# Index logits of a sparse-attention layer: three rounded products of split operands in place of fp32 products

## The chip, the cores and the metric

One core of a Trainium2 chip runs the whole program. The metric is the device time of one execution in microseconds. Three runs of the kernel before gave 2183.99, 2184.31 and 2185.58 us, median 2184.31 us; a fourth execution, taken by the hardware profiler, took 2184.07 us and its trace spans 2182.3 us from the first to the last instruction. All rows below come from that fourth execution.

## The reference, cut to what matters

The program is a two-layer decoder trunk over 512 tokens of width 1024: feed-forward blocks, a gated linear attention beside a state-space mixer in layer 0, a sparse attention in layer 1 (the odd layer), cross attention and a final norm. The change touches one line of the odd layer's mixer, the index logits:

```python
q, k, v, qi, ki, wi = jnp.split(hn @ w_in, _splits(OD_SIZES), axis=-1)
qi = apply_rope(qi.reshape(Bsz, L, IDX_HEADS, IDX_DIM), cos_i, sin_i)   # 8 heads of 64
ki = apply_rope(ki.reshape(Bsz, L, 1, IDX_DIM), cos_i, sin_i)[:, :, 0]   # one key head
# for each block of 128 queries:
logits = jnp.einsum('bqhd,bsd->bqhs', qib, ki)
score = jnp.einsum('bqhs,bqh->bqs', jax.nn.relu(logits), wib)
score = jnp.where(kpos <= tq, score, -jnp.inf)
_, idx = lax.top_k(score, 128)
```

The scores decide which 128 keys each query sees. Queries of the first block (0 to 127) see all their keys, so logits are computed for the query blocks 1, 2 and 3 only.

## The kernel before, in words

Every large product of the program is made of three products of rounded operands ("fp32r"): a weight w is split into a high part (rounded) and a low part (w minus the high part), the activations x likewise, and `mm3` (L431 to L435) adds high·high, high·low and low·high in PSUM. GpSimd (POOL) splits the weights: for each half of a 128x1024 weight block it makes the high part (L387, a tensor_scalar) and the low part (L394, a subtraction of two SBUF operands). It may split a half of block b once TensorE has done with the same half of block b-2, since there are two slots. Scalar engine (ACT) and Vector engine (DVE) split the activations.

The input projections of the odd layer are 15 "tiles" u = 0 to 14 in the order of `OD_ORDER`: u = 0 is the index key (tile 14, stored twice, in rows 0 to 63 and 64 to 127), u = 1 to 4 are the index queries (tiles 10 to 13, two heads of 64 rows each), u = 5 to 14 are the attention's queries and keys. `tile` runs 8 chunks k = 0 to 7 of three matmuls each, and `beside(k)` puts other work ahead of a chunk.

- The projection goes to a PSUM bank. ACT's `swap(u)` (L1535) copies it with halves exchanged into another bank, DVE's `od_out(u)` multiplies by cosine and sine (L2304, L2305) and adds (L2309) into `Pt[t]` in the arena in SBUF: that is the rotary embedding, and the add increments `rope_done`.
- TensorE's `logit_pair(j)` (L921 to L930) stands ahead of chunk 1 and chunk 5 of the tiles u = 3 to 8, twelve pairs in all. A pair is two fp32 products for two heads of one query block, the one on rows 0 to 63, the other on rows 64 to 127, into banks 0 and 1. By `LOGITS` the widths are 512, 384, 512, 384, 512, 384, 512, 384, 256, 256, 256, 256 keys. Pairs 0 and 1 use the query tile of u = 1, pairs 2 and 3 that of u = 2, pairs 4 and 5 of u = 3, pairs 6 and 7 of u = 4. A pair waits for its tile's `rope_done` and for `idx_acc`, the sums of the pair before.
- ACT's `relu_pair` (L1543) applies the relu in place, DVE's `add_logit` (L2325, L2328) multiplies by the head's weight and adds into the score.
- On ACT the order of one round u is: relu of the even pair of tile u+1, `swap(u)`, relu of the odd pair of tile u+1. In round 0 the four copies of the attention's values (L1556) follow, each of which increments `od_v`; tile u = 2 on TensorE waits for the first of them, tiles 3 to 5 for one more each, since they take over those banks.
- On DVE the order of one round is: two `add_logit`, the two multiplications of `od_out`, two `add_logit`, the add. In round 0 the folding of the rotary table (L2295, L2296) and a copy of the mask (L2367) follow; from u = 5 on, rounds of the top-k search (L2344, L2345).

The order of work is written out by hand, each engine runs its own list, and semaphores join them.

Of the kernel before, what the change touches and what calls it, by code (L numbers as in the profile page):

```python
# [28 lines left out]
F32 = mybir.dt.float32  # L29
F32R = mybir.dt.float32r  # L30
I32 = mybir.dt.int32
ALU = mybir.AluOpType
ACT = mybir.ActivationFunctionType
AX = mybir.AxisListType

P = 128
T = 512
# [57 lines left out]
def od_bank(u):  # L95

    return [1, 0][u] if u < 2 else BANKS[u % 4 - 2]
# [74 lines left out]
OD_ORDER = [14, 10, 11, 12, 13] + list(range(10))  # L172
# [59 lines left out]
def build_trunk(nc, xT, memT, pos, vecs, w_alpha, s5b, s5bt, s5c, blocks, mats, mask, rows, stream, out):  # L232
    with ExitStack() as ctx:  # L233
        def sb(name, shape, dt=F32):
            return ctx.enter_context(nc.sbuf_tensor(name, shape, dt))
# [3 lines left out]
        def S(name):  # L239
            if name not in sems:  # L240
                sems[name] = ctx.enter_context(nc.semaphore(name))
            return sems[name]

        ps = ctx.enter_context(nc.psum_tensor("ps", [P, 8, T], F32))
        h = sb("h", [P, KC, T])
        X = [sb(f"x{i}", [P, KC, 2, T], F32R) for i in range(2)]
# [26 lines left out]
        Pt = [ar[:, i * T:(i + 1) * T] for i in range(16)]  # L273
# [6 lines left out]
        def area(at, n=T):  # L280
            return ar[:, at:at + n]
# [19 lines left out]
        def by_offset(x):  # L301

            return x.rearrange("p (s k) -> p k s", s=STRIDE)
        od_val = area(A_ODV, 2 * T).rearrange("p (t d) -> p t d", t=4)

        def split_p(hd, mc, part):

            return X[hd // 2][:, 4 + 2 * (hd % 2) + mc, part, :]
# [121 lines left out]
        def _(pe):  # L430
# [490 lines left out]
            def logit_pair(j):  # L921
                qb, first = LOGITS[2 * j]
                nk = (qb + 1) * P
                pe.wait_ge(S("rope_done"), first // 2 + 2)
                if j >= 1:
                    pe.wait_ge(S("idx_acc"), 2 * j)
                for e in range(2):
                    r = slice(64 * e, 64 * e + 64)
                    pe.matmul(ps[:, e, 0:nk], Pt[10 + first // 2][r, qb * P:(qb + 1) * P],
                              Pt[14][r, 0:nk], start=True, stop=True).then_inc(S("logit_mm"), 1)  # L930

            def odd_inputs():

# [237 lines left out]
        def _(act):  # L1171
# [352 lines left out]
            def swap(u):  # L1524

                i, b = u, od_bank(u)
                n = 64 if OD_ORDER[u] < 10 else 32
                act.wait_ge(S("block_done"), od_block(u) + 1)
                if i >= 2:
                    act.wait_ge(S("rope_done"), i - 1)  # L1530
                if i == 1:
                    act.wait_ge(S("rcol_ready"), 2)
                for at in range(0, P, 2 * n):
                    for lo, up in ((at, at + n), (at + n, at)):
                        m = act.activation(ps[lo:lo + n, 6 + i % 2, :], ps[up:up + n, b, :], ACT.Copy)  # L1535
                m.then_inc(S("rope_s"), 1)

            def odd_inputs():
                def relu_pair(j):
                    for i in (2 * j, 2 * j + 1):  # L1540
                        nk = (LOGITS[i][0] + 1) * P
                        act.wait_ge(S("logit_mm"), i + 1)
                        act.activation(ps[:, i % 2, 0:nk], ps[:, i % 2, 0:nk], ACT.Relu).then_inc(S("relu"), 1)  # L1543

                for u in range(OD_TILES):
                    j = 2 * (u + 1 - LOGIT_TILES[0])
                    if u + 1 in LOGIT_TILES:
                        relu_pair(j)
                    swap(u)
                    if u + 1 in LOGIT_TILES:  # L1550
                        relu_pair(j + 1)
                    if u == 0:
                        act.wait_ge(S("rcol_ready"), 2)
                        for tt in range(4):
                            act.wait_ge(S("wi_ready"), tt + 1)
                            act.activation(od_val[:, tt, :], ps[:, BANKS[tt], 0:2 * P],  # L1556
                                           ACT.Copy, scale=col[:, 16 + tt:17 + tt]).then_inc(S("od_v"), 1)
# [130 lines left out]
            ffn(2, lambda: memory_split(1))  # L1688
            norm(5)
            odd_inputs()  # L1690
            kv_next[0] = 0
            attention(lambda n: fill(1, n))
# [12 lines left out]
        def _(dve):  # L1705
            step = [0]

            def chain(ins):

                step[0] += 1  # L1710
                ins.then_inc(S("dve_step"), 1)
                dve.wait_ge(S("dve_step"), step[0])
# [187 lines left out]
            def rstd_columns(l):  # L1900
                dve.wait_ge(S("rcol_mm"), l + 1)
                dve.tensor_copy(col[:, 16:20], ps[:, RCOL_BANK[l], :].rearrange("p (t n) -> p t n", n=P)[:, :, 0]
                                ).then_inc(S("rcol_ready"), 1)
                dve.wait_ge(S("rcol_ready"), l + 1)
# [384 lines left out]
            def fold(kind):  # L2289

                if kind == 2:
                    dve.wait_ge(S("tab"), 4)
                sign = vec[:, V_SIGNA + kind // 2:V_SIGNA + kind // 2 + 1]
                c, s = area(A_TAB + kind * T), area(A_TAB + (kind + 1) * T)
                dve.tensor_tensor(c, c, rstd[:], ALU.mult)  # L2295
                chain(dve.scalar_tensor_tensor(s, s, sign, rstd[:], ALU.mult, ALU.mult))  # L2296

            def od_out(u, between=None):

                t, src = OD_ORDER[u], ps[:, od_bank(u), :]  # L2300
                i, kind = u, 0 if t < 10 else 2
                turned = ps[:, 6 + i % 2, :]
                dve.wait_ge(S("rope_s"), i + 1)
                dve.tensor_tensor(Pt[t], src, area(A_TAB + kind * T), ALU.mult).then_inc(S("proj_out"), 1)  # L2304
                chain(dve.tensor_tensor(turned, turned, area(A_TAB + (kind + 1) * T), ALU.mult))  # L2305
                if between is not None:
                    between()
                dve.wait_ge(S("proj_out"), OD_BASE + u + 1)
                dve.tensor_tensor(Pt[t], Pt[t], turned, ALU.add).then_inc(S("rope_done"), 1)  # L2309

            def indexer_weights():
                for tt in range(4):
                    dve.tensor_scalar(col[:, 32 + 8 * tt:40 + 8 * tt], ps[:, BANKS[tt], 2 * P:2 * P + WI],
                                      col[:, 16 + tt:17 + tt], (IDX_HEADS * IDX_DIM) ** -0.5, ALU.mult, ALU.mult
                                      ).then_inc(S("wi_ready"), 1)
                dve.wait_ge(S("wi_ready"), 4)

            def add_logit(i):
                qb, hd = LOGITS[i]
                nk = (qb + 1) * P  # L2320
                sc, x = area(A_SC + qb * T)[:, 0:nk], ps[:, i % 2, 0:nk]
                w = col[:, 32 + 8 * qb + hd:33 + 8 * qb + hd]
                dve.wait_ge(S("relu"), i + 1)
                if hd == 0:
                    ins = dve.tensor_scalar(sc, x, w, None, ALU.mult)  # L2325
                else:
                    dve.wait_ge(S("idx_acc"), i)
                    ins = dve.scalar_tensor_tensor(sc, x, w, sc, ALU.mult, ALU.add)  # L2328
                ins.then_inc(S("idx_acc"), 1)
                if hd == IDX_HEADS - 1:  # L2330
                    dve.wait_ge(S("idx_acc"), i + 1)
                    chain(dve.tensor_tensor(sc[:, qb * P:nk], sc[:, qb * P:nk], cmask, ALU.add))
# [18 lines left out]
            def odd_inputs():  # L2351
                fold(2)
                rstd_columns(1)
                indexer_weights()
                for u in range(OD_TILES):
                    first = 4 * (u + 1 - LOGIT_TILES[0])
                    if u + 1 in LOGIT_TILES:
                        add_logit(first)
                        add_logit(first + 1)
                    def later_pair():  # L2360
                        add_logit(first + 2)
                        add_logit(first + 3)

                    od_out(u, later_pair if u + 1 in LOGIT_TILES else None)
                    if u == 0:
                        fold(0)
                        chain(dve.tensor_copy(area(A_SC)[:, 0:P], cmask))  # L2367
                    if u + 1 in LOGIT_TILES:
                        if u >= 5:
                            topk(1)  # L2370
                    elif 8 <= u < 14:
                        topk(2)
# [282 lines left out]
```

## Time and profile before

| what | value |
|---|---|
| median of three runs | 2184.31 us |
| profiled execution: time, span | 2184.07 us, 2182.3 us |
| TensorE (PE) busy | 2169.7 us, 99% of the span |
| weight loads (PEld) busy | 1793.2 us, 82% |
| GpSimd (POOL) busy | 1533.1 us, 70% |
| Vector (DVE) busy | 1045.5 us, 48% |
| Scalar (ACT) busy | 452.1 us, 21% |
| TensorE in the logit pairs (L929) | 11.0 us busy in 48 records, from 1482.4 to 1525.4 us |

In this trace an fp32 matmul leaves two records and an fp32r matmul one, so a logit pair shows as four. A matmul record lasts from its start to the modelled end of its results, and records overlap; what a matmul costs TensorE is the distance from one start to the next. Times in the rows are microseconds from the start of the span.

### The profile page before, as it was taken

How to read it: one execution, taken by the hardware profiler on the slowest of the kernel's cores; microseconds unless marked ns; L12 is line 12 of the kernel's file. 1: busy time of each engine (PE TensorE's matmuls, PEld its weight loads, DVE VectorE, ACT ScalarE, POOL GpSimd, SP SyncE). 2: the span in 40 equal slices, each digit the busy share in tenths (PEclk: the TensorE clock that was granted, in tenths of full speed). 3: DMA queues.
4: the chain of work that ended last, by engine and by line, in shares of the span. 5: the costliest groups of instructions: out<-in, count | busy, mean ns of one | idle time of the engine just before them, and what ended most of it. 6: DMA issues, size and time to landing. Idle time of an engine off the chain costs nothing. (4 is left out here: it accounts for less than half of the span.)

```text
span 2182.3 us, 30340 instructions
## 1 busy us (share of the span) xinstructions
PE 2169.7 (99%) x10582; PEld 1793.2 (82%) x10582; DVE 1045.5 (48%) x1386; ACT 452.1 (21%) x808; POOL 1533.1 (70%) x1538
## 2 busy tenths in 40 slices
PE   9999999999999999999999999999999999999998
PEld 7888888888888888888888888886878888888887
DVE  6556795695444352233363224346872543222333
ACT  3101212034123210001131111134362332111112
POOL 7777787667964776676777667675756657666764
PEclk9999999999999999999999999999999999999999
DMA  5333333223331323323333333232322223332232
GB/s 193 96 96 115 115 98 122 88 78 98 126 97 54 102 97 96 97 96 97 114 97 96 96 97 97 98 99 77 106 88 92 77 65 95 97 96 97 99 97 82
DMA packets 115350, 214.12 MB, mean 98 GB/s; under 512 B 12832, under 2 KB 14400, under 8 KB 115008
## 3 DMA queue, kind: packets, MB, share of 16 engines
q1 hardware_dynamic: 111024, 202.03, 29.1%
q10 hardware_dynamic: 4240, 10.99, 1.5%
q8 instruction: 49, 0.80, 0.2%
q14 instruction: 37, 0.30, 0.0%
HBM read 208.77 MB, written 4.19 MB: 98 GB/s over the span
## 5 line engine op out<-in xcount | busy, mean ns | idle before, releaser
L433 PE MATMUL ps<-x,w_split 128*128 128x512 f32 (+1 forms) x2854 | 1105.7, 387 | 3.4 <-POOL w_split L394 1.8
L435 PE MATMUL ps<-x,w_split 128*128 128x512 f32 (+1 forms) x2854 | 1097.1, 384 | 0.0
L434 PE MATMUL ps<-x,w_split 128*128 128x512 f32 (+1 forms) x2854 | 1096.9, 384 | 0.0
L394 POOL TENSOR_TENSOR w_split<-w_raw,w_split 128x512 fp32r<-128x512 f32 x758 | 1024.7, 1352 | 63.3
L387 POOL TENSOR_SCALAR w_split<-w_raw 128x512 fp32r<-128x512 f32 x758 | 498.5, 658 | 562.0 <-PE ps L435 555.2
L433 PEld LDWEIGHTS ps<-x,w_split 128*128 128x128 f32 x2854 | 536.0, 188 | 121.9 <-issue 10.5
L434 PEld LDWEIGHTS ps<-x,w_split 128*128 128x128 f32 x2854 | 536.2, 188 | 106.6 <-issue 1.4
L435 PEld LDWEIGHTS ps<-x,w_split 128*128 128x128 f32 x2854 | 536.1, 188 | 106.6
L1854 DVE TENSOR_TENSOR x<-arena,x 128x512 fp32r<-128x512 f32 x88 | 118.6, 1358 | 219.1 <-ACT x L1306 219.1
L1804 DVE TENSOR_TENSOR tu<-ps,rstd 128x512 f32<-128x512 f32 x88 | 60.7, 689 | 315.7 <-PE ps L435 315.7
L1244 ACT ACTIVATE sg<-tg 128x512 f32<-128x512 f32 x88 | 55.6, 632 | 669.9 <-DVE tg L1801 668.7
L1801 DVE TENSOR_TENSOR tg<-ps,rstd 128x512 f32<-128x512 f32 x88 | 60.6, 689 | 175.2 <-PE ps L435 174.5
L1810 DVE TENSOR_TENSOR arena<-sg,tu 128x512 f32 (+1 forms) x88 | 119.7, 1360 | 17.9 <-ACT sg L1244 9.8
L1306 ACT ACTIVATE x<-arena 128x512 fp32r (+1 forms) x88 | 54.2, 629 | 348.4 <-PE ps L435 348.0
L1769 DVE SCALAR_TENSOR_TENSOR h<-ps,h 128x512 f32<-128x512 f32 x63 | 43.2, 686 | 166.2 <-PE ps L435 165.9
L1174 ACT ACTIVATE x<-h,vec 128x512 fp32r<-128x512 f32 x64 | 46.0, 723 | 221.2 <-DVE h L1769 173.8
L1727 DVE SCALAR_TENSOR_TENSOR x<-h,vec,x 128x512 fp32r<-128x512 f32 x64 | 60.4, 947 | 27.3 <-ACT x L1174 27.3
L433 PE MATMUL ps<-w_split,x 128*128 128x256 f32 (+2 forms) x192 | 59.8, 312 | 0.4 <-POOL w_split L394 0.3
L435 PE MATMUL ps<-w_split,x 128*128 128x256 f32 (+2 forms) x192 | 57.7, 301 | 0.0
L434 PE MATMUL ps<-w_split,x 128*128 128x256 f32 (+2 forms) x192 | 57.6, 300 | 0.0
L1785 DVE RECIPROCAL rstd<-std 128x512 f32<-128x512 f32 x8 | 26.8, 3354 | 53.0 <-ACT std L1234 53.0
L1211 ACT ACTIVATE sq<-h 128x512 f32<-128x512 f32 x63 | 38.9, 618 | 15.2 <-DVE h L1769 15.2
(301 smaller groups left out, 1329.3 us busy)
## 6 DMA issues: line engine op xcount, KB each, us to landing
w_raw<-in_stream SPq DMA_DIRECT2D x758, 256.0 KB, 2.6
arena<-in_memT ACTq DMA_DIRECT2D x2, 1024.0 KB, 4.9
s_tables<-kv ACTq DMA_DIRECT2D x4, 512.0 KB, 3.2
arena<-s_tables ACTq DMA_DIRECT2D x4, 512.0 KB, 4.5
out<-h ACTq DMA_DIRECT2D x6, 256.0 KB, 2.3
h<-in_xT SPq DMA_DIRECT2D x4, 256.0 KB, 5.4
h<-in_xT SPq DMA_DIRECT2D x2, 512.0 KB, 7.0
w_raw<-in_stream SPq DMA_DIRECT2D x5, 128.0 KB, 5.9
```

The costliest lines, as they stand in the source:

```text
L387: pool.tensor_scalar(W[:, s, 0, c], raw[:, s, c], 1.0, 0.0, ALU.mult, ALU.add).then_inc(S(f"w_hi{'ab'[half]}"), 1)
L394: pool.tensor_tensor(lo, x, hi.bitcast(F32), ALU.subtract).then_inc(split_ready if half else S("half_split"), 1)
L433: pe.matmul(dst, wh, xh, start=start, stop=False)
L434: pe.matmul(dst, wh, xl, start=False, stop=False)
L435: return pe.matmul(dst, wl, xh, start=False, stop=stop)
L1244: act.activation(sg[:, s, :], tg[:, s, :], ACT.Silu).then_inc(S("silu"), 1)
L1306: act.activation(X[xo][:, ch:ch + 1, 0, :], hid[:, d, :], ACT.Copy).then_inc(S("x_hi"), 1)
L1727: dve.scalar_tensor_tensor(X[to][:, k, 1, :], h[:, k, :], gain(n, k), X[to][:, k, 0, :].bitcast(F32), ALU.mult, ALU.subtract).then_inc(S(" ...
L1801: dve.tensor_tensor(tg[:, s, :], ps[:, BANKS[2 * s], :], rstd[:], ALU.mult).then_inc(S("gate_ready"), 1)
L1804: dve.tensor_tensor(tu[:, s, :], ps[:, BANKS[2 * s + 1], :], rstd[:], ALU.mult).then_inc(S("up_ready"), 1)
L1810: dve.tensor_tensor(dst, sg[:, s:s + 1, :], tu[:, s:s + 1, :], ALU.mult).then_inc(S("hid_done"), 1)
L1854: dve.tensor_tensor(X[xo][:, ch:ch + 1, 1, :], hid[:, d, :], X[xo][:, ch:ch + 1, 0, :].bitcast(F32), ALU.subtract).then_inc(S("x_lo"), 1)
```

## The change

It touches three places. TensorE's `logit_pair` waits for a new semaphore `idx_lo` in place of `rope_done`, and makes six fp32r matmuls of a pair in place of two fp32 ones: three products (high·high, low·high, high·low) for each of the two heads, heads alternating. The operands are the high and low parts of the index keys and queries, kept in `X[0]`, of which the queries hold only the 384 columns of the blocks 1 to 3. ACT makes the high part in rounds u = 0 to 4, after the relus of the round, as a copy from the arena once the tile's `rope_done` has come; in round 0 it stands ahead of the four value copies. DVE makes the low part as a subtraction of two SBUF operands, after `od_out(u)`, once the high part is there.

```diff
+        def index_split(t, part):
+            x = X[0][:, 0:4, :, :].rearrange("p a b t -> p (a b t)")
+            if t == 14:
+                return x[:, part * T:(part + 1) * T]
+            at = 2 * T + ((t - 10) * 2 + part) * 3 * P
+            return x[:, at:at + 3 * P]
+
+        def index_tile(t):
+            return Pt[t] if t == 14 else Pt[t][:, P:T]
...
             def logit_pair(j):
                 qb, first = LOGITS[2 * j]
                 nk = (qb + 1) * P
-                pe.wait_ge(S("rope_done"), first // 2 + 2)
+                pe.wait_ge(S("idx_lo"), first // 2 + 2)
                 if j >= 1:
                     pe.wait_ge(S("idx_acc"), 2 * j)
-                for e in range(2):
-                    r = slice(64 * e, 64 * e + 64)
-                    pe.matmul(ps[:, e, 0:nk], Pt[10 + first // 2][r, qb * P:(qb + 1) * P],
-                              Pt[14][r, 0:nk], start=True, stop=True).then_inc(S("logit_mm"), 1)
+                for i, (pq, pk) in enumerate(((0, 0), (1, 0), (0, 1))):
+                    for e in range(2):
+                        r = slice(64 * e, 64 * e + 64)
+                        m = pe.matmul(ps[:, e, 0:nk], index_split(10 + first // 2, pq)[r, (qb - 1) * P:qb * P],
+                                      index_split(14, pk)[r, 0:nk], start=(i == 0), stop=(i == 2))
+                        if i == 2:
+                            m.then_inc(S("logit_mm"), 1)
...
                     if u + 1 in LOGIT_TILES:
                         relu_pair(j + 1)
+                    if u < 5:
+                        act.wait_ge(S("rope_done"), u + 1)
+                        act.activation(index_split(OD_ORDER[u], 0), index_tile(OD_ORDER[u]), ACT.Copy
+                                       ).then_inc(S("idx_hi"), 1)
                     if u == 0:
                         act.wait_ge(S("rcol_ready"), 2)
                         for tt in range(4):
...
                     od_out(u, later_pair if u + 1 in LOGIT_TILES else None)
+                    if u < 5:
+                        t = OD_ORDER[u]
+                        dve.wait_ge(S("idx_hi"), u + 1)
+                        dve.tensor_tensor(index_split(t, 1), index_tile(t), index_split(t, 0).bitcast(F32), ALU.subtract
+                                          ).then_inc(S("idx_lo"), 1)
                     if u == 0:
                         fold(0)
```

How the lists of instructions change. Lines of the changed kernel have other numbers: L1550 is the swap (L1535 before), L1558 the relu (L1543), L1575 the value copies (L1556), L1569 the new copy; L2387 is the new subtraction, L2328 the rotary add (L2309 before), L2323 and L2324 the rotary multiplications.

On the Scalar engine before, from the swap of u = 0 to the relus of pair 2:

```order
334 L1535 ACTIVATE ps<-ps 32x512 [waits block_done]
335 L1535 ACTIVATE ps<-ps 32x512 x3
336 L1556 ACTIVATE arena<-ps,col 128x256 [waits wi_ready,rcol_ready]
337 L1556 ACTIVATE arena<-ps,col 128x256 [waits wi_ready] x3
338 L1535 ACTIVATE ps<-ps 32x512 [waits rcol_ready,block_done]
339 L1535 ACTIVATE ps<-ps 32x512 x3
340 L1543 ACTIVATE ps<-ps 128x512 [waits logit_mm] x2
341 L1535 ACTIVATE ps<-ps 32x512 [waits rope_done,block_done]
342 L1535 ACTIVATE ps<-ps 32x512 x3
343 L1543 ACTIVATE ps<-ps 128x384 [waits logit_mm] x2
344 L1543 ACTIVATE ps<-ps 128x512 [waits logit_mm] x2
```

The same stretch in the changed kernel:

```order
334 L1550 ACTIVATE ps<-ps 32x512 [waits block_done]
335 L1550 ACTIVATE ps<-ps 32x512 x3
336 L1569 ACTIVATE x<-arena 128x512 [waits rope_done]
337 L1575 ACTIVATE arena<-ps,col 128x256 [waits wi_ready,rcol_ready]
338 L1575 ACTIVATE arena<-ps,col 128x256 [waits wi_ready] x3
339 L1550 ACTIVATE ps<-ps 32x512 [waits rcol_ready,block_done]
340 L1550 ACTIVATE ps<-ps 32x512 x3
341 L1569 ACTIVATE x<-arena 128x384 [waits rope_done]
342 L1558 ACTIVATE ps<-ps 128x512 [waits logit_mm] x2
343 L1550 ACTIVATE ps<-ps 32x512 [waits rope_done,block_done]
344 L1550 ACTIVATE ps<-ps 32x512 x3
345 L1558 ACTIVATE ps<-ps 128x384 [waits logit_mm] x2
```

The first new copy waits for the rotary add of the key and stands ahead of the value copies; the copy of u = 2 comes next after the last row shown, behind the relus of pair 1.

On the Vector engine in the changed kernel, from the rotary add of u = 0 to the subtraction of u = 2:

```order
706 L2328 TENSOR_TENSOR arena<-arena,ps 128x512 [waits proj_out,dve_step]
707 L2387 TENSOR_TENSOR x<-arena,x 128x512 [waits idx_hi]
708 L2314 TENSOR_TENSOR arena<-arena,rstd 128x512
709 L2315 SCALAR_TENSOR_TENSOR arena<-arena,vec,rstd 128x512
710 L2391 COPY arena<-mat 128x128 [waits dve_step]
711 L2323 TENSOR_TENSOR arena<-ps,arena 128x512 [waits rope_s,dve_step]
712 L2324 TENSOR_TENSOR ps<-ps,arena 128x512
713 L2328 TENSOR_TENSOR arena<-arena,ps 128x512 [waits proj_out,dve_step]
714 L2387 TENSOR_TENSOR x<-arena,x 128x384 [waits idx_hi]
715 L2344 TENSOR_SCALAR arena<-ps,col 128x512 [waits relu]
```

Before, the rows were the same without the two of L2387. In rounds 2 to 4 the subtraction follows the add in the same way and is the last instruction of the round.

## Rows read from the trace of the kernel before

**Rows 1.** The page: busy time by engine, then the granted clock in 40 slices.

```profile
PE 2169.7 (99%) x10582; PEld 1793.2 (82%) x10582; DVE 1045.5 (48%) x1386; ACT 452.1 (21%) x808; POOL 1533.1 (70%) x1538
...
PEclk9999999999999999999999999999999999999999
```

**Rows 2.** Timeline, PE, pair 0 (512 keys): start, length, engine, line, operation.

```profile
1482.04 0.39 PE L435 MATMUL ps<-x,w_split 128*128 128x512 f32 x1
1482.36 1.13 PE L929 MATMUL ps<-arena 64*128 64x512 f32 x4
1483.42 0.50 PE L433 MATMUL ps<-x,w_split 128*128 128x512 f32 x1
1483.75 0.39 PE L434 MATMUL ps<-x,w_split 128*128 128x512 f32 x1
```

**Rows 3.** Timeline, PE, pairs 1 (384 keys), 2 and 11 (256 keys).

```profile
1486.38 0.92 PE L929 MATMUL ps<-arena 64*128 64x384 f32 x4
1487.22 0.50 PE L433 MATMUL ps<-x,w_split 128*128 128x512 f32 x1
...
1489.87 0.39 PE L435 MATMUL ps<-x,w_split 128*128 128x512 f32 x1
1490.26 0.70 PE L929 MATMUL ps<-arena 64*128 64x512 f32 x2
...
1524.65 0.70 PE L929 MATMUL ps<-arena 64*128 64x256 f32 x4
1525.28 0.50 PE L433 MATMUL ps<-x,w_split 128*128 128x512 f32 x1
```

**Rows 4.** Timeline, PE, a run of fp32r matmuls of 256 columns.

```profile
1620.42 0.28 PE L433 MATMUL ps<-w_split,x 128*128 128x256 f32 x1
...
1622.81 0.28 PE L435 MATMUL ps<-w_split,x 128*128 128x256 f32 x1
```

**Rows 5.** Waits of PEld: who was waited for, us in total, times, longest.

```profile
PEld ps L929 <- DVE arena L2309: 1.3, 3, 0.4
```

**Rows 6.** Timeline, PE, the first matmul of tile u = 2.

```profile
1476.15 0.39 PE L433 MATMUL ps<-x,w_split 128*128 128x512 f32 x1
```

**Rows 7.** Timeline, ACT, u = 0 to the relus of pair 1; then line L1306.

```profile
1474.16 1.57 ACT L1556 ACTIVATE arena<-ps,col 128x256 f32<-128x256 f32 x4 [1.46 <-DVE col L2313]
1476.35 2.29 ACT L1535 ACTIVATE ps<-ps 32x512 f32<-32x512 f32 x4 [0.62 <-PE ps L435]
...
1487.32 0.86 ACT L1543 ACTIVATE ps<-ps 128x384 f32<-128x384 f32 x2 [0.42 <-PE ps L929]
...
L1306 ACT ACTIVATE x<-arena x88: 615/632/634, 243.1 to 2148.0; 128x512 fp32r x64, 128x512 fp32r<-128x512 f32 x24
```

**Rows 8.** Timeline, DVE, u = 0 to 1, and the end of round 2.

```profile
1475.83 0.69 DVE L2309 TENSOR_TENSOR arena<-arena,ps 128x512 f32<-128x512 f32 x1
1476.43 0.68 DVE L2295 TENSOR_TENSOR arena<-arena,rstd 128x512 f32<-128x512 f32 x1
...
1479.40 0.69 DVE L2304 TENSOR_TENSOR arena<-ps,arena 128x512 f32<-128x512 f32 x1
...
1480.73 0.69 DVE L2309 TENSOR_TENSOR arena<-arena,ps 128x512 f32<-128x512 f32 x1
...
1489.53 0.68 DVE L2309 TENSOR_TENSOR arena<-arena,ps 128x512 f32<-128x512 f32 x1
```

**Rows 9.** Timeline, POOL, the split beside pair 2.

```profile
1489.73 0.62 POOL L387 TENSOR_SCALAR w_split<-w_raw 128x512 fp32r<-128x512 f32 x1 [1.82 <-PE ps L435]
1490.44 1.26 POOL L394 TENSOR_TENSOR w_split<-w_raw,w_split 128x512 fp32r<-128x512 f32 x1
```

**Rows 10.** Line L1854 on DVE (ns min/median/max); then DVE and POOL timelines, one collision.

```profile
L1854 DVE TENSOR_TENSOR x<-arena,x x88: 677/1772/1784, 243.8 to 2148.6; 128x512 fp32r<-128x512 f32 x88
...
2099.90 1.78 DVE L1854 TENSOR_TENSOR x<-arena,x 128x512 fp32r<-128x512 f32 x1 [3.66 <-ACT x L1306]
...
2099.85 1.28 POOL L394 TENSOR_TENSOR w_split<-w_raw,w_split 128x512 fp32r<-128x512 f32 x1
```

## The prediction

> **What bounds the kernel now.** I read the busy times first: TensorE is busy for 99% of the span at a granted clock of nine tenths or more in every slice [rows 1]. So almost every us that TensorE loses is a us of the time, and an engine at 48% (DVE) or 21% (ACT) costs nothing until TensorE has to wait for it. Next I read the TensorE timeline around the logit pairs, since the change lives there. A full fp32r matmul of 512 columns costs 0.2265 us from start to start (26 steps from 1476.15 to 1482.04) [rows 2, 6]; one of 256 columns costs 0.1195 us (20 steps) [rows 4]. Last I read who keeps TensorE waiting there: PEld waited for the rotary add L2309 three times, 0.4 us each [rows 5]. Part of that is the usual gap: the step from the last fp32r matmul to pair 0 is 0.32 us, to pair 2 it is 0.39 us [rows 2, 3]. The real wait before pairs 2, 4 and 6 is thus near 0.1 us each, 0.3 us in all. It is small, but it says that **the chain through relu, score sums and rotary add already ends last at those three pairs**. What the change puts behind that add comes straight onto TensorE's path.
>
> **Part 1: the matmuls of a pair.** Before, pair 0 takes 0.32 us to switch in, 1.06 us from its start to the next matmul, then 0.33 us for a step that otherwise takes 0.23 [rows 2]. The 1.06 us are 0.84 at 384 keys and 0.63 at 256 [rows 3]. The two differences, 0.22 and 0.21 us for 128 columns each, say 1.7 ns for a column: four passes at 2.4 GHz (the higher level of the clock), and four, not eight, because the two heads on rows 0 to 63 and 64 to 127 run side by side. What is left is a fixed 0.20 us. After, there are six one-pass matmuls. If the halves run side by side too, these are three rounds at 0.2265, 0.17 (between the two measured widths) and 0.1195 us; with the same 0.20 us a pair has 0.88, 0.71 and 0.56 us, which saves 0.18, 0.13 and 0.07 us. Four pairs of each: **-1.5 us in all**. No half-row fp32r matmul is in the trace, so I bound it from both sides. Good end: the 0.10 us of the slow step behind a pair go too, another 1.2 us, so -2.7. Bad end: no side-by-side at all, six matmuls of 0.2265, 0.17 and 0.1195 us plus 0.20, which is 1.56, 1.22 and 0.92 us and costs 0.50, 0.38 and 0.29 more, **+4.7 us** over twelve pairs. I take -1.5, since the fp32 halves on the same rows do overlap.
>
> Here a page speaks against the forecast. The Trainium skill, "TensorE: Matmul & The Clock Gate", section "The mechanism", says that a weight load overlaps matmuls in flight only where the row group differs; the six matmuls load each row group three times, so by that rule two loads of each pair would be exposed. The 0.10 us of late start behind a pair is the nearest measure of one exposed load [rows 2]; with it a mechanism of its own follows, the fifth case below.
>
> **Part 2: the key's copy and subtraction (u = 0).** The first copy of ACT waits for the rotary add of the key, which ends at 1475.83 + 0.69 = 1476.52 [rows 8]. It is 512 columns SBUF to SBUF, 0.63 us as L1306 [rows 7]: done 1477.19. Queued behind it are the four value copies, 0.39 us each, which started at 1474.16 [rows 7] and now start at 1477.19. The first is done at 1477.58. Tile u = 2 needs it and began at 1476.15 [rows 6]; it now begins near 1477.6. **+1.5 us.** The next three value copies are wanted a tile later each, and cost nothing. POOL is late by nothing: its splits wait for TensorE.
>
> **Part 3: pair 0 waits for the query of u = 1.** ACT: the last value copy ends 1478.75, swap(1) takes 2.29 us [rows 7], until 1481.05. DVE: the key's subtraction starts at 1477.2; what followed the add took from 1476.43 to 1479.40 [rows 8], 2.97 us, so DVE is there at about 1480.9 if the subtraction takes 0.7 us, and 1481.7 if it stands behind POOL. Then the two multiplications and the add, 1479.40 to 1481.42 [rows 8], 2.02 us: 1483.1. Copy of 384 columns: 0.63 minus about 0.11 (the relu's 1.07 us for two of 512 against 0.86 for two of 384), so 0.53: 1483.65. Subtraction, 0.56 alone: 1484.3, with a short wait behind POOL's L387 1484.45. TensorE is ready for the pair at 1482.36 + 1.5 = 1483.85. **+0.7 us**, and +2.0 if either subtraction falls behind a whole L394.
>
> **Part 4: pairs 2, 4 and 6.** This is the largest term. In round u of DVE the rotary add ends the chain; pair 1 starts at 1486.38, the add of round 2 ends at 1489.53 + 0.68 = 1490.21, pair 2 starts at 1490.26 [rows 3, 8]. Behind the add now come the copy on ACT (0.04 of signal, 0.53) and the subtraction on DVE. The pair itself is 0.13 us shorter. So the subtraction can start at 1490.21 + 0.04 + 0.53 + 0.04 - 0.13 = 1490.69 on the old scale, while TensorE would be ready at 1490.17 - 0.13 = 1490.04. That is 0.65 us late already. And POOL is in the way: its L394 runs from 1490.44 to 1491.70 [rows 9], released by the end of tile u, 0.13 less on the same scale, 1490.31 to 1491.57. Both subtractions read two SBUF operands. What happens then is in the trace: L1854, the same instruction at 512 columns, takes 0.68 us alone and 1.77 us in the median; the one at 2099.90 began 0.05 us behind an L394 of 1.28 us, and ended 0.55 us after it [rows 10]. So the new subtraction waits until 1491.57, ends 0.45 us later (384 columns), 1492.02, and TensorE starts at 1492.07: 2.0 us after it was ready. The same phases repeat for pairs 4 and 6, because POOL and the chain both hang on the same tile. **3 x 2.0 = +6.1 us**, in place of the 0.3 us waited now. Were there no collision, the subtraction would end at 1491.25 and a wait would be 1.25 us, 3.8 us in all.
>
> A page gives the rule for this row: the Trainium skill, "SBUF — State Buffer", section "Who interferes with whom", says that a DVE instruction with two SBUF inputs and a GpSimd instruction that reads SBUF exclude each other, the later one blocked entirely, and that issue order decides. The row agrees (1.78 us); by the opposite order DVE would pay nothing.
>
> **Part 5: what is free.** Pairs 8 to 11 and the odd ones use tiles that were split before: no new wait. The five copies and subtractions, some 3 and 3 to 6 us of work, fill engines that now stand idle, outside the places counted. No DMA is added. POOL may be held up by a subtraction for up to 0.7 us, against 1.82 us for which it sat idle before such a split [rows 9]. Later stages start late by the same amount on all engines, and nothing is made up, since TensorE is the bound.
>
> **Sum.** +1.5 +0.7 +6.1 -0.3 -1.5 = **+6.5 us** on the profiled execution's 2184.07 us (span 2182.3), that is 2190.6 us. That execution is 0.24 us under the median of the three runs, 2184.31, against which I read faster and slower; it makes +6.3.
>
> **Rivals.**
> 1. Forecast: slower by about 6 us, 2190.6. Chance 0.55.
> 2. The waits come but the port collision does not, because DVE gets there first or the phases shift, and the switch behind a pair gets cheap: 6.5 - 2.3 - 1.2 = +3.0, 2187.1. For: the phase margin between copy and L394 is a few tenths of a us. Against: 1.77 us is the median of 88 such subtractions [rows 10]. Chance 0.18.
> 3. Half rows don't run side by side in fp32r: the pairs cost +4.7 in place of -1.5, 6.5 + 6.2 = +12.7, 2196.8. For: no such instruction in the trace. Against: the fp32 pairs overlap, and 128 columns cost them 0.21 us, not 0.43. Chance 0.08.
> 4. Faster: the new work lies off the chain altogether, no wait (the 0.3 us go too), and the whole fixed cost of a pair, 0.20 + 0.10 + 0.09 us of switching in, belongs to fp32 and goes: -0.3 - 1.5 - 12 x 0.39 = -6.5, 2177.6. It decides only if the copy and subtraction end before TensorE is ready, which the 0.65 us of part 4 forbid before any collision. Chance 0.05.
> 5. Loads of one row group exposed twice a pair: 12 x 0.2 = 2.4 more, 2193.0. Against: full fp32r matmuls load the same rows each time and still step at 0.2265 us. Chance 0.09.
> 6. The change saves the pair's time but hardly costs: chain as in 2 with single waits hidden, within 3 us of before. Chance 0.05.
>
> **How the numbers follow.** 0.2% is 4.4 us, about what a measurement of this kernel can tell from no change: slower is above 2188.7. Cases 1, 3 and 5 are above, with a little taken off for case 1's lower tail: 0.72 - 0.02 = 0.70, and a fifth of case 2: 0.73 in all. Case 4 gives faster, 0.05. The rest, 0.22, is no change. The range: its low end is case 2's, 2187.0; its high end is 2195.0, over case 5 with pair 0's longer wait (+1.3), and leaves case 3 out. Some 0.1 lies below and 0.1 above.
>
> **What would show it.** Right: TensorE idle near 1.5 us at the first matmul of tile u = 2; an idle of about 2 us before pairs 2, 4 and 6 put down to L2387; L2387 at 384 columns lasting over 1 us in rounds 2 to 4, with an L394 beside it; a pair of 512 from its start to the next matmul at 0.88 us. The forecast is wrong if L2387 lasts 0.56 us there (case 2), if a pair takes 1.5 us (case 3), or if TensorE doesn't wait at those places (cases 4 and 6). If the granted clock falls to 1.2 GHz behind one of the waits, which no wait of up to 2 us in this trace tests in that stretch, every matmul there takes twice as long and the time is some us above the sum.

## The result and the profile after

The changed kernel took 2192.91 us (median of seven runs, 2191.47 to 2194.73) against 2184.54 us for the kernel before in the same seven rounds (2183.99 to 2186.07): 1.0038 times, 95% interval 1.0028 to 1.0047, or 8.4 us more. The forecast was 2190.6 us, range 2187 to 2195, slower. The profiled execution is one of 2192.91 us with a span of 2191.1 us.

On the page the busy times hardly move: TensorE 2172.5 us, still 99%, and DVE 1050.8 against 1045.5 [rows 1]. The loss can't be seen there. It is in the waits of TensorE; the first view holds those of the changed kernel (who waits, for whom, us in total, times, longest):

```profile
PE ps L942 <- DVE x L2387: 5.2, 4, 1.9
PE ps L445 <- POOL w_split L406: 1.9, 2, 1.6
PE ps L445 <- ACT arena L1575: 1.5, 1, 1.5
```

The first row is the pairs waiting for the new subtraction, the third is tile u = 2 waiting for the value copies. Before, PE had no wait in this stretch and its weight loads waited 1.3 us for the rotary add [rows 5]. The second row stands before as well, at the start of the program.

The timeline of TensorE, with idle time and its releaser in brackets, answers to [rows 2, 3, 6]:

```profile
1476.09 0.39 PE L447 MATMUL ps<-x,w_split 128*128 128x512 f32 x1
1477.99 0.47 PE L445 MATMUL ps<-x,w_split 128*128 128x512 f32 x1 [1.52 <-ACT arena L1575]
...
1483.99 0.39 PE L447 MATMUL ps<-x,w_split 128*128 128x512 f32 x1
1484.94 0.96 PE L942 MATMUL ps<-x 64*128 64x512 f32 x6 [0.56 <-DVE x L2387]
1485.83 0.50 PE L445 MATMUL ps<-x,w_split 128*128 128x512 f32 x1
...
1488.78 0.79 PE L942 MATMUL ps<-x 64*128 64x384 f32 x6
1489.49 0.50 PE L445 MATMUL ps<-x,w_split 128*128 128x512 f32 x1
...
1492.12 0.39 PE L447 MATMUL ps<-x,w_split 128*128 128x512 f32 x1
1494.43 0.96 PE L942 MATMUL ps<-x 64*128 64x512 f32 x6 [1.92 <-DVE x L2387]
...
1501.61 0.39 PE L447 MATMUL ps<-x,w_split 128*128 128x512 f32 x1
1503.92 1.20 PE L942 MATMUL ps<-x 64*128 64x512 f32 x6 [1.92 <-DVE x L2387]
1505.05 0.79 PE L445 MATMUL ps<-x,w_split 128*128 128x512 f32 x1
1505.64 0.63 PE L446 MATMUL ps<-x,w_split 128*128 128x512 f32 x1
...
1512.66 0.39 PE L447 MATMUL ps<-x,w_split 128*128 128x512 f32 x1
1513.83 0.97 PE L942 MATMUL ps<-x 64*128 64x512 f32 x6 [0.79 <-DVE x L2387]
...
1532.48 0.50 PE L445 MATMUL ps<-x,w_split 128*128 128x512 f32 x1
```

Read steps from start to start, not the bracket alone. The step to tile u = 2 is 1.90 us in place of 0.23: 1.7 us lost. The steps to pairs 0, 2, 4, 6 are 0.95, 2.31, 2.31 and 1.17 us where 0.32 is the plain switch: 0.6, 2.0, 2.0 and 0.85 us lost. A pair itself, from its start to the next matmul, is 0.89 us at 512 keys and 0.71 at 384, against 1.06 and 0.84 [rows 2, 3]. The last line is the matmul behind pair 11, 7.2 us later than before (1525.28) [rows 3].

Behind pair 4 the matmuls step at 0.43 us, not 0.23. The granted clock of these stretches (columns: stretch, length, busy time of the five engines, clock, DMA share, GB/s) says why:

```profile
1502.00:1504.00 2.00, 0.08 (x2) 0.09 (x2) 1.27 (x2) 0.52 (x1) 1.36 (x2) 1.00 0.00 0
1504.00:1506.00 2.00, 2.00 (x8) 1.23 (x9) 0.24 (x1) 0.85 (x2) 0.00 (x0) 0.61 0.50 131
1506.00:1508.00 2.00, 2.00 (x6) 1.54 (x5) 1.26 (x2) 1.94 (x5) 0.00 (x0) 0.53 0.00 0
1508.00:1510.00 2.00, 2.00 (x12) 1.24 (x11) 1.30 (x2) 0.54 (x1) 1.08 (x2) 1.00 0.00 0
```

TensorE idled from 1502.0 to 1503.9. It then still had the full clock until about 1504.4 (0.91 in the stretch from 1504.25 to 1504.5), and the lower level, 1.2 GHz, until about 1507.9 (0.50 from 1505 to 1507.5). From pair 4 to pair 5 it took 5.38 us, from pair 0 to pair 1 3.84: 1.5 us lost. Then the wait at pair 6 came out shorter. The rotary adds and subtractions of rounds 2 and 4 on DVE, and their neighbours on POOL, in the changed kernel:

```profile
1491.95 0.68 DVE L2328 TENSOR_TENSOR arena<-arena,ps 128x512 f32<-128x512 f32 x1
1493.21 1.16 DVE L2387 TENSOR_TENSOR x<-arena,x 128x384 fp32r<-128x384 f32 x1 [0.59 <-ACT x L1569]
...
1511.95 0.68 DVE L2328 TENSOR_TENSOR arena<-arena,ps 128x512 f32<-128x512 f32 x1
1513.22 0.56 DVE L2387 TENSOR_TENSOR x<-arena,x 128x384 fp32r<-128x384 f32 x1 [0.59 <-ACT x L1569]
...
1492.69 1.26 POOL L406 TENSOR_TENSOR w_split<-w_raw,w_split 128x512 fp32r<-128x512 f32 x1
...
1513.23 1.69 POOL L406 TENSOR_TENSOR w_split<-w_raw,w_split 128x512 fp32r<-128x512 f32 x1
```

In round 2 POOL came first, by 0.52 us, and DVE's subtraction lasted 1.16 us; in round 4, after the slow clock, DVE was first by 0.01 us: its subtraction took 0.56 us and POOL's stretched from 1.26 to 1.69. That is 0.6 us of the 1.1 by which the step to pair 6 is shorter (1.17 against 2.31). The other 0.5 comes from the chain itself. The slow clock held up TensorE alone, so DVE had its two multiplications of the round done before pair 5's relus came, and began pair 5's score sums 1.39 us after the pair's start (1510.69 against 1509.30) where it was 1.91 us behind pair 1 (1490.69 against 1488.78). The rotary add thus starts 0.71 us ahead of TensorE's last matmul before pair 6, and only 0.17 us ahead of the one before pair 2.

The books of the profiled execution, in us: +1.7 (tile u = 2), +0.6, +2.0, +2.0, +0.85 (pairs 0, 2, 4, 6), +1.5 (clock), -0.3 (old waits), -1.5 (twelve pairs, 0.17, 0.13 and 0.08 each) make 6.85. The two traces are 7.2 us apart at the norm behind this stretch (mean-square matmuls at 1714.8 against 1707.6) and 0.2 at the one ahead (1466.5 against 1466.3), so 7.0 us arise between. The rest of the 8.8 us between the spans is in the last microseconds of the program, the sixteen small matmuls of the final norm, first the changed kernel, then the one before:

```profile
2180.13 3.66 PE L484 MATMUL ps<-mat,col 128*128 128x128 f32 x16
```

```profile
2172.90 2.05 PE L472 MATMUL ps<-mat,col 128*128 128x128 f32 x16
```

The same matmuls take 1.6 us more at the lower clock (granted 0.50 from 2181 to 2183 us; 1.00 from 2173 to 2175 in the kernel before), in code that the change doesn't touch. Among the profiles of the experiments below, x4's has the same fall at the final norm (3.45 us), all others take 2.05 us there. A fall can come elsewhere too. The profile of x11, which has no copy and no subtraction, was taken of an execution 1.8 us over that kernel's lowest, and has its fall near 25 us, behind a wait for a split weight:

```profile
24.23 0.50 PE L433 MATMUL ps<-x,w_split 128*128 128x512 f32 x1 [1.77 <-POOL w_split L394]
24.57 0.41 PE L434 MATMUL ps<-x,w_split 128*128 128x512 f32 x1
24.81 0.59 PE L435 MATMUL ps<-x,w_split 128*128 128x512 f32 x1
25.20 0.63 PE L433 MATMUL ps<-x,w_split 128*128 128x512 f32 x1
```

The kernel before waits 1.84 us at the same place and its profile has no fall. So falls of some 1.5 us each come in some executions and not in others, which fits the groups some 1.5 us apart in which the times of one kernel lie (2191.5, 2192.6 to 2193.0, 2194.5 to 2194.7 here). No profile of the kernel before caught an execution of its upper groups, so for that kernel it is not shown.

### The profile page after: what moved, and what is told of

It reads as the page before. It is cut to its first block and busy times, and to the rows that moved or that the text cites. A ratio compares the mean times of both kernels' runs of the same rounds, so it can differ in the third digit from the quotient of the medians.

```text
span 2191.1 us, 30398 instructions
## 1 busy us (share of the span) xinstructions
PE 2172.5 (99%) x10606; PEld 1798.0 (82%) x10606; DVE 1050.8 (48%) x1391; ACT 454.9 (21%) x813; POOL 1535.8 (70%) x1538
```

## The experiments

Eleven kernels besides. My theory: the products save 1.5 us; all of the loss is TensorE waiting for operands that the chain relu, score sums, rotary add, copy, subtraction delivers late, made worse by the collision with POOL's subtraction and by the clock behind a wait. Rivals: the half-row products themselves cost; the copies and subtractions cost wherever they stand.

**x1_products_alone: the new matmuls, nothing else.** The kernel before with

```diff
-                    pe.matmul(ps[:, e, 0:nk], Pt[10 + first // 2][r, qb * P:(qb + 1) * P], Pt[14][r, 0:nk], ...)
+                for i, (pq, pk) in enumerate(((0, 0), (1, 0), (0, 1))):
+                    for e in range(2): ...
+                        m = pe.matmul(ps[:, e, 0:nk], X[1][r, 0, pq, (qb - 1) * P:qb * P], X[1][r, 1, pk, 0:nk], ...)
```

> The kernel before with the six half-row rounded products of a pair, but on other operands that lie ready (parts of the projection's input), behind the old wait for the rotary add; no copies, no subtractions. The logits are therefore not the index logits. It prices the matmuls alone. My account (the pair's time is one pass of four less, the chain untouched): pairs of 0.89, 0.71 and 0.54 us to the next matmul in place of 1.06, 0.84 and 0.63, the waits before pairs 2, 4, 6 the same 0.1 us, together -1.5 us: 2183.0, ratio 0.9993. Rival (half rows cost more in their new form than fp32, and the trace of the changed kernel hides it in its waits): +0 to +5 us.

2183.41 us, ratio 0.9994 (0.9985 to 1.0003), before 2185.08 in the same session. The interval holds no change; the trace is what prices it. Its pair 0 (timeline, TensorE):

```profile
1482.42 0.39 PE L435 MATMUL ps<-x,w_split 128*128 128x512 f32 x1
1482.74 0.97 PE L930 MATMUL ps<-x 64*128 64x512 f32 x6
1483.64 0.50 PE L433 MATMUL ps<-x,w_split 128*128 128x512 f32 x1
1483.98 0.40 PE L434 MATMUL ps<-x,w_split 128*128 128x512 f32 x1
```

0.32 us in, 0.90 to the next, then 0.34: the fixed costs of the fp32 pair stayed, one pass of four went. The products are no part of the loss, as I expected. The waits did not stay the same, though: the steps to pairs 2, 4 and 6 are 0.56, 0.52 and 0.56 us where the kernel before has 0.39 to 0.41, so 0.4 of the 1.5 us comes back as waiting for the rotary add. No run follows that up.

**x2_waits_alone: the new waits, old matmuls.** The changed kernel with the fp32 lines put back under the wait for `idx_lo`.

```diff
-                for i, (pq, pk) in enumerate(((0, 0), (1, 0), (0, 1))): ...
+                for e in range(2): ...
+                    pe.matmul(ps[:, e, 0:nk], Pt[10 + first // 2][r, qb * P:(qb + 1) * P], Pt[14][r, 0:nk], ...)
```

> The changed kernel with the old fp32 pairs, but behind the new waits, with all copies and subtractions. My account (all of the loss is the chain): the loss of the changed kernel plus the 1.5 us of the pairs, +8 to +11 us by whether the clock falls behind a wait, ratio 1.004 to 1.005; 2 us of wait before pairs 2 and 4. Rival (the split products themselves cost): clearly less than the changed kernel, near +3.

2193.59 us, ratio 1.0041 (1.0027 to 1.0055). Pairs 2, 4 and 6 now all wait the full length:

```profile
1477.85 0.47 PE L445 MATMUL ps<-x,w_split 128*128 128x512 f32 x1 [1.52 <-ACT arena L1572]
1484.81 1.13 PE L941 MATMUL ps<-arena 64*128 64x512 f32 x4 [0.56 <-DVE x L2384]
...
1494.62 1.13 PE L941 MATMUL ps<-arena 64*128 64x512 f32 x4 [1.92 <-DVE x L2384]
...
1504.43 1.13 PE L941 MATMUL ps<-arena 64*128 64x512 f32 x4 [1.92 <-DVE x L2384]
...
1514.22 1.13 PE L941 MATMUL ps<-arena 64*128 64x512 f32 x4 [1.91 <-DVE x L2384]
```

The waits alone give the whole loss; "clearly less than the changed kernel" did not come. With all waits in place and a granted clock of 1.00 through this stretch the profiled run took 2192.25 us, 8.2 us over the profiled run of the kernel before; by steps the waits make 1.7 + 0.6 + 3 x 2.0 - 0.3 = 8.0.

**x3_values_first: the key's copy behind the value copies.**

```diff
-                    if u < 5: ... act.activation(index_split(OD_ORDER[u], 0), index_tile(OD_ORDER[u]), ACT.Copy)
                     if u == 0: ... four value copies
+                    if u < 5: ... act.activation(index_split(OD_ORDER[u], 0), index_tile(OD_ORDER[u]), ACT.Copy)
```

> The changed kernel with the four value copies ahead of the key's copy on the Scalar engine. My account: the first matmul of tile u = 2 follows its predecessor by 0.23 us as before, -1.6 us; pairs 2, 4, 6 wait as in the changed kernel, 2191.3. Rival (tile u = 2 waits for something else, the port or the bank): no change at tile u = 2.

2193.68 us, ratio 1.0039 (1.0026 to 1.0053), where I had expected 2191.3: a miss. Tile u = 2 starts without a wait, as expected, but the next wait took it all:

```profile
1485.71 0.96 PE L942 MATMUL ps<-x 64*128 64x512 f32 x6 [2.67 <-DVE x L2387]
```

Pair 0 waits 2.67 us in place of 0.56. TensorE came 1.7 us sooner, its operands didn't; and POOL, released sooner too, now ran into DVE's work of round 0 (1.09 and 1.20 us in this version against 0.74 and 0.23 us in the changed kernel for the second table instruction and the mask copy). The two are waits on one chain, and I had read the first as a price of its own. Its profile also has two falls of the clock, behind this wait (granted 0.50 from 1488 to 1490 us) and behind the 1.92 us before pair 6.

**x4_sum_in_psum: one SBUF operand in the subtraction.** The rotary sum of the index tiles stays in PSUM.

```diff
-                dve.tensor_tensor(Pt[t], Pt[t], turned, ALU.add).then_inc(S("rope_done"), 1)
+                dve.tensor_tensor(turned if u < 5 else Pt[t], Pt[t], turned, ALU.add).then_inc(S("rope_done"), 1)
-            return Pt[t] if t == 14 else Pt[t][:, P:T]
+            return ps[:, 6 + u % 2, 0 if u == 0 else P:T]
-                    act.wait_ge(S("rope_done"), i - 1)
+                    act.wait_ge(S("idx_lo") if i < 7 else S("rope_done"), i - 1)
```

> The changed kernel, but the rotary sum of the five index tiles is left in PSUM, so that the new subtraction has only one SBUF operand; the bank is held until the subtraction is done. Account with the shared read port: the subtraction takes 0.56 us (384 columns) everywhere although POOL's subtraction runs beside it, the waits before pairs 2 and 4 fall from 1.9 to about 1.1 us idle, -1.5 us, and if the clock then stays up another -1.5: 2190 to 2191.5. Rival (the subtraction was slow for another reason, such as the write to X): it stays at 1.16 us in rounds 2 and 3, no change.

2189.97 us (eleven runs, 2188.48 to 2192.31), ratio 1.0023 (1.0014 to 1.0032). The new subtraction in both kernels, ns shortest, median and longest, here and in the changed kernel:

```profile
L2387 DVE TENSOR_TENSOR x<-ps,x x5: 557/558/691, 1477.5 to 1510.5; 128x384 fp32r<-128x384 f32 x4, 128x512 fp32r<-128x512 f32 x1
```

```profile
L2387 DVE TENSOR_TENSOR x<-arena,x x5: 559/1158/1780, 1477.4 to 1513.2; 128x384 fp32r<-128x384 f32 x4, 128x512 fp32r<-128x512 f32 x1
```

The write to X is the same in both, so it isn't what was slow: two SBUF operands beside POOL's reading is. POOL was as busy beside it as before: in round 2 of x4 its subtraction ran from 1492.32 for 1.26 us, and DVE's from 1492.77 for 0.56 us inside it. The waits before pairs 2, 4 and 6 fell to 1.25, 1.30 and 1.29 us, and the median is 2.9 us under that of the changed kernel (two sessions; the ratios are 1.0023 and 1.0038).

**x5_both: x3 and x4 together.**

> Value copies first and the rotary sum of the index tiles in PSUM. Account: tile u = 2 starts without a wait (0.23 us); the key's subtraction no longer collides (1.78 to 0.6 us), so pair 0 waits for about 1.3 us in place of the 2.7 us with the value copies first alone; pairs 2, 4, 6 wait 1.25 to 1.3 us each. With no clock fall 2188.0, about 0.5 to 1 us under the version with the sum in PSUM alone. Rival (waits just move): the same time as that version, 2190.

2188.34 us, ratio 1.0016 (1.0006 to 1.0025). Waits of 1.03, 1.25, 1.29 and 1.30 us before pairs 0, 2, 4, 6 and none at tile u = 2. Without that collision the value copies' order is worth something after all, about 1 us from its lowest run to that of x4 (2187.39 against 2188.48).

**x6_head_by_head: three products of one head, then three of the other.**

```diff
-                for i, (pq, pk) in enumerate(...):
-                    for e in range(2):
+                for e in range(2):
+                    for i, (pq, pk) in enumerate(...):
```

> The changed kernel with the six matmuls of a pair in another order: three products of the first head (rows 0 to 63), then three of the second (rows 64 to 127). Account A (the two halves run side by side in any order, as the two records of each fp32 product did): a pair takes 0.89 us at 512 keys as before. Account B (side by side only when neighbours in the queue alternate): the pair takes about five slots of 0.2265 in place of three, 1.35 us, and the time rises by up to 4 us.

2192.87 us, ratio 1.0036 (1.0023 to 1.005). Account A: a pair of 512 keys takes 0.90 us to the next matmul against 0.89, one of 384 keys 0.72 against 0.71.

```profile
1489.08 0.79 PE L942 MATMUL ps<-x 64*128 64x384 f32 x6
1489.80 0.50 PE L445 MATMUL ps<-x,w_split 128*128 128x512 f32 x1
```

**x7_filled: matmuls of no use in the waits.**

```diff
+                if j in (2, 4, 6):
+                    for _ in range(6):
+                        pe.matmul(ps[:, 0, :], ones_r[:], X[1][:, 0, 0, :], start=True, stop=True)
                 pe.wait_ge(S("idx_lo"), first // 2 + 2)
```

> The changed kernel with six rounded matmuls of 512 columns, of no use for the result, before each of the pairs 2, 4 and 6, into bank 0 which the pair then overwrites: they fill the waits for the subtraction (6 x 0.2265 = 1.4 us of the 1.9 us). My account of the clock: it falls in the changed kernel where TensorE sat idle before; with the wait filled the granted clock stays 1.00 there and the falls' 1.5 us are saved, 2191.4. Rival (the falls have nothing to do with the waits): the granted clock falls as often and the time stays 2192.9.

2191.30 us (2190.87 to 2193.24), ratio 1.0030 (1.0018 to 1.0043). TensorE idles 0.56 us at most before each late pair, and the granted clock stays up (columns as above):

```profile
1500.00:1510.00 10.00, 9.45 (x46) 6.81 (x45) 6.25 (x10) 4.71 (x9) 3.82 (x4) 1.00 0.18 52
```

Five of its six runs lie within 2190.87 to 2191.36, where those of the changed kernel spread over 3.3 us. That speaks for the waits as the cause of the falls, but the intervals of the two ratios overlap, and x2 had the same waits without a fall in its profile. Over all thirteen profiles TensorE idles for 1.45 us or more 29 times, and the clock fell within 2 us of the end of six of these waits (one in the changed kernel, two in x3, one each in x6, x8 and x11). While TensorE had work, the only other falls are the two at the final norm, with no such wait ahead. The link is supported, not settled.

**x8_tile_later: all pairs one tile later.** With the value copies first, and two top-k rounds moved to the start of the attention:

```diff
-LOGIT_TILES = range(3, 9)
+LOGIT_TILES = range(4, 10)
-                        if u >= 5:
+                        if u >= 6:
-                    elif 8 <= u < 14:
+                    elif 9 <= u < 14:
-                topk(5)
+                topk(7)
```

> The changed kernel with the twelve pairs one tile later (tiles u = 4 to 9 in place of 3 to 8), the value copies ahead of the key's copy, and two of the top-k rounds moved from the projections to the start of the attention. Copies, subtractions and their collisions stay. My account (all of the loss is that TensorE comes for the split operands before they are there): no wait before any pair, only the 1.5 us of the pairs left, and the 0.3 us of old waits gone: 2182.8, ratio 0.9992, if the Vector engine still has the top-k done when the attention asks. Rival (the copies and subtractions cost by themselves, through POOL's port and the weights' splits): still slower than before by some us.

2186.29 us, ratio 1.0006 (0.9997 to 1.0015) where the changed kernel has 1.0038 in its own session, but short of the 2182.8 that I had expected. No pair waits for its split operands. Pairs 1 and 2 start 0.14 and 0.21 us late (steps of 0.46 and 0.53 us), and one new wait stands where the attention turns its weights, since DVE now had two top-k rounds more to do there. In this profile the clock fell behind it too (granted 0.50 from 1584 to 1587 us):

```profile
PE ps L1001 <- ACT arena L1596: 1.6, 1, 1.6
```

**x9_topk_kept and x10_topk_kept_psum.** As x8, with all fifteen top-k rounds back in the projections; the second also with the sum in PSUM.

```diff
                         if u >= 6:
-                            topk(1)
+                            topk(min(u - 5, 2))
...
-                topk(7)
+                topk(5)
```

> Pairs one tile later and value copies first, as in the version before it, but all fifteen top-k rounds stay in the projections (one at u = 6, two in each of u = 7 to 13). Account (the 1.6 us wait at the attention's transposes came from the two rounds moved there): no wait before the pairs and none at the transposes, 2183.0, ratio 0.999. Rival (the Vector engine is late by its five subtractions and by their collisions with POOL, wherever the top-k stands): the wait at the transposes stays over 1 us, 2185 to 2186.

> The same with the rotary sum of the index tiles in PSUM, so that the subtractions don't collide with POOL. Account: as without it, 2183.0, since nothing waits for them any more; if the Vector engine is still late at the attention, this one is under the other by what the wait there shrinks.

2183.16 us (2182.42 to 2184.98), ratio 0.9995 (0.9986 to 1.0004), and 2182.54 us (2182.24 to 2184.42), ratio 0.9991 (0.9982 to 1.0). Neither waits for split operands or at the transposes. In x9 pairs 1 and 2 still start 0.14 and 0.21 us late: pair 1 starts at 1491.83, just behind the score sums of pair 0, which end at 1491.68. In x10 all twelve steps are 0.31 or 0.32 us. The lowest of eleven runs, 2182.24, is 1.7 us under the lowest of 27 of the kernel before, 2183.94. Both intervals still touch 1, so a gain is not shown by the times; if there is one, it is of 1.5 to 2 us, which would be the 1.5 us of the products and the 0.3 us of the old waits.

**x11_fp32_tile_later: the move without the split.** The kernel before with fp32 pairs and the top-k as in x9.

```diff
-LOGIT_TILES = range(3, 9)
+LOGIT_TILES = range(4, 10)
```

> The kernel before (fp32 pairs, no copies, no subtractions) with its pairs one tile later and the same placing of the top-k: what the move gives without the split. Account: the 0.3 us of waits before pairs 2, 4 and 6 go, 2184.2 on this measure, ratio 0.9999; the split products then are worth the other 1.5 us. Rival (the move itself is what gains or loses): clearly off the kernel before, by 1 us or more.

2184.23 us, ratio 0.9998 (0.9989 to 1.0007): the same as before, though the steps to pairs 2, 4 and 6 are now 0.32 us. What x9 and x10 are below it, 1.5 and 1.7 us by the lowest runs, fits the 1.5 us of the split products; the intervals overlap here too.

## Why the prediction was right, and where it was off

The sign, the mechanism and the places were right; the sum of 6.5 us was 1.9 us short of the 8.4 us measured.

- **Products (part 1), -1.5.** Measured -1.5 in the books, alone in x1 with the same steps. The good end (the slow step behind a pair goes) did not come: the step is 0.34 us. Case 3 and case 5 are out by x1 and x6: half rows run side by side as rounded products in either order.
- **Value copies (part 2), +1.5.** Measured 1.7: idle 1.52 and a slow second step. But x3 shows that it isn't a price of its own. Taking the wait away gave pair 0 2.1 us more idle. The prediction's sum is not hurt by that, since part 3 counts from a TensorE that is already 1.5 us late; it was my expectation for x3 that took the 1.5 us as a gain to be had alone.
- **Pair 0 (part 3), +0.7.** 0.6. The key's subtraction did fall behind POOL (1.78 us), and the slack in DVE's round 0 absorbed it: with DVE's table work late, it missed POOL and took 0.74 and 0.23 us where it had taken 1.1 and 1.2. So the +2.0 that part 3 names for a subtraction behind a whole POOL subtraction did not follow.
- **Pairs 2, 4, 6 (part 4), +6.1.** 2.0, 2.0 and 0.85 in the profiled run; 2.0 each in x2, where the clock stayed. That "the same phases repeat" failed at pair 6, behind the slow clock. The collision was real: x4 removed it and a wait fell by 0.65 us. The uncollided wait of 1.25 us was near too: 1.25 to 1.30 us idle in x4, 1.3 to 1.4 us by the steps. The rule of issue order (the Trainium skill, "SBUF — State Buffer", "Who interferes with whom") showed itself in round 4, where DVE was first and paid nothing: 0.56 us.
- **What the sum lacked: the clock.** I named a fall behind a wait of 2 us as what would put the time "some us above the sum" and gave it no price. It cost 1.5 us behind pair 4, of which pair 6 gave back 1.1 (0.6 by the missed collision, 0.5 by the chain that had caught up). So it is in part luck that the terms of part 4 add up as forecast in this profile. And it cost 1.6 us at the final norm. Without any fall the books give 1.7 + 0.6 + 3 x 2.0 - 0.3 - 1.5 = 6.5 us; the median is 8.4, and a fall behind a wait (0.4 net) and one at the final norm (1.6) are the difference in the profiled run. Why the final norm had one in the profiled run of this kernel and not in that of before is open: nothing there changed but the time at which it runs, and no wait stands ahead of it.
- **Rival 2** needed the collision to stay away and the switch behind a pair to get cheap. The collision came, and the switch stayed at 0.34 us; x4, with the collision taken out, is still 4.9 us over the kernel before by the medians. **Rivals 4 and 6** needed the operands to be there in time, which took a move of all pairs (x9, x10); the fixed costs that rival 4 lets go stayed even there.

## What to carry to other kernels

Fewer passes on the bound engine are worth their passes only if the operands come in time: a pass of 0.2 us was bought with 1.2 us of copy and subtraction at the end of a chain that had 0.1 us of wait already. Read the slack of the consumer first, and move the consumer (here by one tile) along with the new producer; then check what the move takes room from, here the top-k. And don't take a wait's length for what its removal gives: x3 took 1.7 us out, and the next wait of the same chain grew by 2.1.

## What the runs showed of the hardware that I had not expected

- Half-row rounded products share the array whichever way they are queued: 0.72 us for six of 384 columns head by head, 0.71 alternating (x6).
- A rounded half-row pair keeps the fixed costs of the fp32 pair, 0.32 us in and 0.34 us for the second step behind it (x1). So they are not a price of fp32 alone. That they belong to the switch between half rows and full rows is my reading; no run tests it.
- In the changed kernel an idle of 1.92 us was followed by the lower clock behind pair 4 (from about 1504.4 to 1507.9 us) and by no fall behind pair 2; x2 had three such idles and no fall, x6 one behind the third (granted clock of 1510 to 1520: 0.83).
- Who comes first decides the whole price of the collision: with POOL 0.52 us ahead DVE's subtraction took 1.16 us, with DVE 0.01 us ahead it took 0.56 us and POOL's 1.69 in place of 1.26.
